# A two-layer encoder trunk on one core: recurrence levels in 32-column blocks, and weight splits in another order

## The reference

```python
def hgrn2(h, w_in, lb, o_norm_g, w_out):
    q, f, i, g = jnp.split(h @ w_in, 4, axis=-1)
    forget = lb + (1.0 - lb) * jax.nn.sigmoid(f)
    k, q = 1.0 - forget, jax.nn.silu(q)
    # S_t = diag(f_t) S_{t-1} + k_t i_t^T,  o_t = S_t^T q_t, with 8 heads of 128
    ...
    return (rms_norm(o) * jax.nn.silu(g)) @ w_out

def moe_swiglu(h, w_router, b_router, w_gu, w_down):
    # the two best of 8 experts for each token
    for e in range(N_EXPERTS):
        out = out + gates[..., e:e + 1] * swiglu(h, w_gu[e], w_down[e])   # E_FF = 3584
```

## Time and profile before

| | us |
|---|---|
| median of 3 runs | 1499.53 (1497.72 to 1499.70) |
| the profiled execution | 1497.92 |
| its span | 1496.2 |
| PE busy | 1465.4 |
| DVE busy | 1237.6 |
| ACT busy | 1004.9 |

### The profile page before, as it was taken

One profiled execution on the slowest core, in us unless ns is written; L12 is line 12 of the kernel. 1 busy time (PEld: TensorE's weight loads), 2 busy tenths in 40 slices (PEclk: granted clock), 3 DMA queues, 4 the chain that ended last, 5 costly groups with the idle time before them and its releaser, 6 DMA issues.

```text
span 1496.2 us, 23664 instructions
## 1 busy us (share of the span) xinstructions
PE 1465.4 (98%) x6903; PEld 1215.8 (81%) x6903; DVE 1237.6 (83%) x1556; ACT 1004.9 (67%) x1248; POOL 45.9 (3%) x43
## 2 busy tenths in 40 slices
PE   8999999999999999999999999999999999999998
PEld 6877888788887778888888888888888888888876
DVE  7996545674778899899989989889989889899985
ACT  6555434366236677787877877777787778778762
POOL 1000000000000120000000000000000000000000
PEclk9999999999999999999999999999999999999999
DMA  7666555456233899999999999999989999999960
GB/s 284 210 219 224 188 199 174 168 167 213 74 128 122 299 410 409 346 367 409 347 374 410 356 364 410 387 327 411 403 319 408 409 341 381 409 348 399 410 245 29
DMA packets 124631, 452.57 MB, mean 302 GB/s; under 512 B 13984, under 2 KB 13984, under 8 KB 124592
## 3 DMA queue, kind: packets, MB, share of 16 engines
q1 hardware_dynamic: 119952, 435.25, 77.4%
q0 software_dynamic: 4640, 16.82, 3.1%
HBM read 443.62 MB, written 8.39 MB: 302 GB/s over the span
## 4 chain that ended last, share of the span: by engine, by line
PE 89%; DVE 7%; issue 1%; ACT 1%; DMA 1%; SPq 0%; ACTq 0%; DVEq 0%
PE PS L460 28%; PE PS L462 28%; PE PS L461 28%; DVE w_lo L1362 3%; PE PS L880 2%; DMA raw<-in_w_in_ab 1%; PE PS L511 0%; PE PS L726 0%; DVE SC L1666 0%; PE PS L847 0%; ACT w_hi L984 0%; DVE SC L1685 0%; DVE SC L1686 0%; PE PS L597 0%; PE PS L834 0%
## 5 line engine op out<-in xcount | busy, mean ns | idle before, releaser
L1362 DVE TENSOR_TENSOR w_lo<-raw,w_hi 128x1024 fp32r<-128x1024 f32 x486 | 568.6, 1221 | 31.4 <-ACT w_hi L984 28.4
L460 PE MATMUL PS<-w_hi,xT_hi 128*128 128x512 f32 x1424 | 567.5, 399 | 6.1 <-DVE w_lo L1362 3.4
L462 PE MATMUL PS<-w_lo,xT_hi 128*128 128x512 f32 x1424 | 557.5, 392 | 0.0
L461 PE MATMUL PS<-w_hi,xT_lo 128*128 128x512 f32 x1424 | 556.4, 391 | 0.0
L984 ACT ACTIVATE w_hi<-raw 128x1024 fp32r<-128x1024 f32 x486 | 489.6, 1060 | 73.0 <-PE PS L462 41.8
L1362 DVE TENSOR_TENSOR w_lo<-SC,w_hi 128x1024 fp32r<-128x1024 f32 x340 | 392.0, 1220 | 8.4 <-ACT w_hi L984 6.8
L984 ACT ACTIVATE w_hi<-SC 128x1024 fp32r<-128x1024 f32 x340 | 335.7, 1061 | 12.3 <-PE PS L462 10.3
L460 PEld LDWEIGHTS PS<-w_hi,xT_hi 128*128 128x128 f32 x1424 | 269.5, 189 | 60.7 <-issue 6.3
L462 PEld LDWEIGHTS PS<-w_lo,xT_hi 128*128 128x128 f32 x1424 | 268.6, 189 | 57.8
L461 PEld LDWEIGHTS PS<-w_hi,xT_lo 128*128 128x128 f32 x1424 | 269.2, 189 | 52.9
L460 PE MATMUL PS<-w_hi,hT_hi 128*128 128x512 f32 x536 | 209.1, 390 | 3.2 <-DVE hT_lo L1580 3.2
(11 more groups left out here) (270 smaller groups left out, 625.8 us busy)
## 6 DMA issues: line engine op xcount, KB each, us to landing
raw<-in_e_w_gu SPq DMA_DIRECT2D x226, 512.0 KB, 8.5
SC<-in_e_w_gu SPq DMA_DIRECT2D x222, 512.0 KB, 8.3
SC<-in_e_w_down SPq DMA_DIRECT2D x114, 512.0 KB, 7.5
raw<-in_e_w_down SPq DMA_DIRECT2D x110, 512.0 KB, 7.8
raw<-in_ffn_w_gu SPq DMA_DIRECT2D x44, 512.0 KB, 4.8
raw<-in_w_in_c SPq DMA_DIRECT2D x32, 512.0 KB, 6.0
raw<-in_ffn_w_down SPq DMA_DIRECT2D x22, 512.0 KB, 5.1
raw<-in_w_in_ab SPq DMA_DIRECT2D x20, 512.0 KB, 8.5
```

Of the source, the lines that this page charges most:

```text
L460: pe.matmul(out, a_hi, b_hi, start=start, stop=False, skip_group_check=True)
L461: pe.matmul(out, a_lo, b_hi, start=False, stop=False, skip_group_check=True)
L462: return pe.matmul(out, a_hi, b_lo, start=False, stop=stop, skip_group_check=True)
L1362: dve.tensor_tensor(w_lo[:, g % RING, part], raw_part(g, s), w_hi[:, g % RING, part].bitcast(F32), ALU.subtract).then_inc(lo_done, 1)
```

## The change

The levels 0 to 5 are cut into four blocks of 32 stationary columns (in the order 0, 64, 32, 96), each with 32 moving columns in level 0 and 16 in levels 1 to 5. The splits of 64 and 65 stand before level 0's merge, 66 behind level 6's update, 67 and 68 behind level 7's, 69 to 72 each where 70 to 73 stood, 73 where 74 stood, and 74 ahead of the first expert's `xg`. In the experts' unit, h is made behind the first of three splits.

```diff
             def level(n):
                 pe.wait_ge(qk_ready, n + 1)
                 for hd in range(HEADS):
                     for t in range(T):
-                        tok = slice(t * P, (t + 1) * P)
-                        if n == 0:
-                            c = (hd % 2) * SEQ + t * P
-                            m = pe.matmul(PS[:, 4 + hd // 2, c:c + P], kT[:, hd, tok], qT[:, hd, tok],
-                                          start=True, stop=True, skip_group_check=True)
+                        if n < 6:
+                            for a in (0, 2 * B, B, 3 * B):
+                                rows, tok = slice(a, a + B), slice(t * P + a, t * P + a + B)
+                                if n == 0:
+                                    c = (hd % 2) * SEQ + t * P + a
+                                    m = pe.matmul(PS[rows, 4 + hd // 2, c:c + B], kT[:, hd, tok], qT[:, hd, tok],
+                                                  start=True, stop=True, skip_group_check=True)
+                                else:
+                                    w = 2 ** (n - 1)
+                                    c = (hd % 4 * T + t) * (P // 2) + a // 2
+                                    m = pe.matmul(
+                                        PS[rows, level_bank(n) + hd // 4, c:c + B // 2].rearrange("p (m w) -> p m w", w=w),
+                                        kT[:, hd, tok], qT[:, hd, tok].rearrange("p (m e w) -> p m e w", e=2, w=w)[:, :, 1, :],
+                                        start=True, stop=True, skip_group_check=True)
...
-            los(62, 64)
+            los(62, 65)
             dve.wait_ge(qT_act, 4)
             dve.sem_inc(qk_ready, 1)
+            lo(65)
...
             meet(0)
             step(dve.tensor_tensor(qT, qT, fT, ALU.mult))
             dve.sem_inc(qk_ready, 1)
-            lo(64)
...
-                if 1 < lv < 7:
-                    lo(63 + lv)
+                if lv == 6:
+                    lo(66)
+            los(67, 69)
...
             norm_o(0)
+            lo(69)
+            gate_o(0)
             lo(70)
-            gate_o(0)
-            lo(71)
...
             gate_o(1)
+            lo(71)
+            xT(1, 4, V_ON)
             lo(72)
-            xT(1, 4, V_ON)
-            lo(73)
...
-            lo(74)
+            lo(73)
...
             select(1)
+            lo(74)
             xg(1)
...
                 def unit(u, end):
-                    for q in (10, 11, 12):
-                        lo(G_MOE + q, i * EU + u)
+                    lo(G_MOE + 10, i * EU + u)
                     unit_hidden(i * EU + u + (FB + 2))
+                    lo(G_MOE + 11, i * EU + u)
+                    lo(G_MOE + 12, i * EU + u)
```

More of the change, by code:

```diff
@@ L697, in turn_heads @@
                         m.then_inc(signal, 1)
+            B = 32
             def level(n):
@@ L722, in level @@
                                               skip_group_check=True)
[L723 to L729, removed]
                 m.then_inc(at_done, 1)
```

## The result

The changed kernel took 1501.32 us in the median against 1498.98 for the kernel before, timed on the same chip: ratio 1.0015, 95% interval 1.0009 to 1.0022, +2.3 us. The interval leaves out 1, so this is a small loss, of 1.3 to 3.3 us; 1501.4 had been forecast. The two profiled executions took 1497.92 before and 1502.34 after (spans 1496.2 and 1500.6, 4.4 apart), so the single profiles differ by 2 us more than the medians do; 0.5 of it is there before the first level already.

A forecast was written before the change was run, and what follows sets the result against it. PE, busy 98% of the span, was taken to bound the kernel. Terms -5.8 (recurrence), -4.3 (first item), +9.1 (item ends) and +2.9 (last unit) sum to +1.9 us: 1501.4 from a median of 1499.53, range 1495.0 to 1507.0.

The forecast's parts named there:

- three signs by which I wanted to be wrong: No wait at the boundaries; PE standing in the levels longer than 1.0 us; PE's granted clock falling inside the levels.
- rival A: Recurrence levels: narrow passes and waits lower PE's clock, +2 to +4 us, hence 1503.5 to 1505.5; chance 0.20.
- Levels: Levels 0 to 5: 2.2 us each instead of 3.49, bounds 1.2 and 3.49; level 7 at 414.0 instead of 424.72.
- rival D: Levels 0 to 5: four column groups side by side, 1.2 us a level, level 7 2.6 earlier, 1498.8; chance 0.10.
- The stall in front of the weighting: Before the weighting of values: PE stands 5.4 us for split 66, load 69, ACT's cast and copies; start 424.3, not 431.13.
- The clock: Behind the stall before the weighting: PE's clock low again, 1.0 us charged, as 12 matmuls lost after the old stall.
- Cost zero: Later splits, 74 ahead of expert 0's xT: covered by 2.25 us of DVE idling; 2.3 were that cover absent.
- First item: Expert stage, first item: h made when split 82 ends, 522.5, ahead of PE's want at 525.1; gain 4.3 us.
- Item ends: Seven expert boundaries: two splits stand between h and the next xT, PE waits 1.3 us each; loss 9.1.
- Last unit: Last expert unit: pT's low part and hT come two splits later, hT ends at 1454.9; loss 2.9 us (2 to 4).
- Rival C: Expert boundaries: no wait for xT, so the 9.1 us loss goes away, 1492.3; chance 0.12.
- Rival B: Levels 0 to 5: nothing saved, 3.49 us each, PE bounds again, level 7 at about 420, 1507.4; chance 0.08.

The follow-up runs named there:

- same_group: Changed kernel with h behind three splits, and in levels 0 to 5 the 16 products of one column block one behind the other: 1502.55 us, ratio 1.0032.
- cast69_later: Changed kernel with ACT's cast of granule 69 behind its copies of levels 6 and 7, not ahead of them: 1495.35 us, ratio 0.9983.
- levels_and_product: Kernel before with the 32-column blocks in levels 0 to 5 and the h placement of three_at_end, splits staying in the levels: 1485.45 us, ratio 0.9911.
- three_cast: three_at_end and cast69_later together: 1482.92 us, ratio 0.9903 against the kernel before.
- split74_behind: three_cast with split 74 behind the tokens of expert 0 on DVE: 1486.39 us, ratio 0.9927 against the kernel before.
- xg_first: Changed kernel with the next expert's xT (in the last unit pT) directly behind h, ahead of two splits: 1499.98 us, ratio 1.0016.
- three_at_end: Changed kernel with h behind one split only in looped units of items before the last, behind three elsewhere: 1485.98 us, ratio 0.9920.
- levels_only: Kernel before with only the 32-column blocks of levels 0 to 5: 1490.64 us, ratio 0.9956.
- splits_only: Kernel before with only the splits moved, levels at 128 columns and h behind three splits: 1500.58 us, ratio 1.0019.

## Why the prediction was right

The time came out within 0.1 us and the difference of the medians as +2.3 for +1.9, and the terms of -5.8, -4.3, +9.1 and +2.9 were measured as -5.2, -4.5, +9.8 and +4.8. Each of the four has the sign and the mechanism that were forecast. The near hit of the sum owes much to luck. The four terms add up to +4.9 and not +1.9, and a cost that I had put at nothing is +1.9 more; two places where the clock happened to do better than before (-1.4 and -1.6) take 3.0 off, one of them tied to that cost. Between the profiles the difference is still +4.4, 2.1 more than between the medians. The base moved too, from 1499.53 (3 runs) to 1498.98 (19).

Two of the three signs by which I wanted to be wrong did show: PE stood in the levels longer than 1.0 (1.69 in front of level 3), and its clock fell inside them (0.74). Neither had the effect that I had tied to it, as the paragraphs on the levels and on rival A show.

**Levels: too long by a factor of 1.8, and little of it reached the total.** I took 2.2 a level from level 6. It was 1.20, my lower bound, the size of rival D: four column groups run side by side (*same_group*). (My 16 ns a pass for level 6 rests on 1.04 us, which the earlier trace rows do not show; their 1.14 makes it 18.) The Trainium skill's sentence on starts no closer than about 25 ns (TensorE: Matmul & The Clock Gate, "Wait — 56ns, not 53.3ns?") does not hold for products in different groups, at 9.4 ns a pass, and stands close to what was measured within one group, 30 ns. Part 3 of the same page, Packing small matmuls, was the section that bore on this case. As far as level 7 rival D was the right one. DVE set the pace around level 3, where PE stood 1.69 and not 1.0, but level 7 came at 412.00 for my 414.0, or 2.5 earlier counted from level 0, where D had 2.6. D's time, 1498.8, did not come because only 1.2 of this reached the weighting, and the clock there cost 1.8 more than I charged (both below).

**The stall in front of the weighting: right mechanism, 6.60 for 5.4.** Split 66 ended at 414.9, 1.5 earlier than forecast, but the second half of load 69 was taken by the cast at 420.31, only 0.6 earlier, since w_out_c now took 5.4 in the median of eight and not the 4.3 of the earlier trace rows. So of D's 2.6 only 0.7 arrived, 1.2 counted from level 0: the weighting began at 423.62 for my 424.3. Why the load was slower was not tried; in the other profiles its median is 4.0 to 5.9. That ACT's cast is the link was shown by *cast69_later*.

**The clock: 1.0 charged, 2.8 measured.** From the weighting's start to the next projection matmul it was 6.26 (423.62 to 429.88), before 3.49 (431.13 to 434.62). I had priced the low clock by the projection's matmuls behind the old stall. Now it fell on the weighting's products, whose first 16 passes show 3.75 and not 1.95. Counted from level 0, the weighting began 1.2 earlier than forecast, which makes up for most of it: -5.2 for -5.8.

**"Cost zero" for split 74: wrong in this profile, +1.9 from gather to first h.** PE waits 1.63 for the tokens, and the clock over the next 9 us is 0.81. The step that failed is the cover. I let the split fill the 2.25 that DVE idled ahead of the tokens, but these belong to a profile whose gather ran at a low clock and took 4.18. Where the gather takes 3.73, as after, only 0.57 are left with the old order (*levels_and_product*), and a split of 2.36 makes the tokens some 1.7 late, an estimate from these rows. Nine profiles have split 74 ahead of the tokens: the two with a gather of 3.73 (after and *three_cast*) show the wait, 1.63 and 1.62, and the seven with one of 3.89 to 5.23 show none. So the +1.9 and most of the -1.4 ahead of the gather belong together: the clock that saved the one laid the split bare. *split74_behind* keeps the split between the gather and the first h and only moves it behind the tokens, where it makes that h late.

**First item: 4.5 for 4.3.** The second turn comes 17.43 after the first and the third 16.84 after that, against 20.23 and 18.53.

**Item ends: 1.40 each for 1.3, 9.8 for 9.1.** The wait for xT is where I put it, 120.65 us apart (the profile's 1.15 counts from the end of the transposes before it). DVE's timeline after, of one item's end:

```profile
601.20 0.69 DVE L1875 TENSOR_TENSOR junk<-junk,PS 128x512 f32<-128x512 f32 x1 [2.78 <-ACT junk L1258]
...
606.34 2.16 DVE L1828 SCALAR_TENSOR_TENSOR xT_lo<-PS,vcol,xT_hi 128x128 fp32r<-128x128 f32 x8
...
622.69 0.69 DVE L1875 TENSOR_TENSOR junk<-junk,PS 128x512 f32<-128x512 f32 x1
```

h starts at 601.20, two splits follow, and the first four of xT end 6.2 later, for the 6.28 of the prediction. What I had not seen is that this is one of two waits with one cause. I worked out that the next h would be ready 22.2 after this h starts and wanted at 22.7; measured 22.2 (622.69 and 0.69, less 601.20) and 22.9 (624.07). That margin existed only because the wait for xT had moved PE back. With xT made first, PE wants h at 21.6 and the loss is 1.2 all the same (*xg_first*). Rival C is refuted for the change, and *three_at_end* shows what it takes to be rid of the loss: the wait for silu must be filled with splits.

**Last unit: 4.8 for 2.9.** hT was made when forecast: its instruction on DVE ends 0.2 before PE takes it at 1456.43, at 1456.2, which less the 1.1 that all stands later there is 1455.1 for my 1454.9. The size failed at the clock: behind the second of two waits, 1.37 and 2.23, the next eight matmuls start 0.43 apart and not 0.23, some 1.6 us. The window after shows the clock (seventh number):

```profile
1456.00:1464.00 8.00, 7.51 (x25) 5.76 (x26) 3.15 (x4) 0.81 (x2) 0.00 (x0) 0.79 0.00 0
```

**Rival A came true in part and cost nothing.** In the profile after the clock over 393 to 399.5 is 0.74. Yet level 4 starts 5.74 behind level 3 (393.67 to 399.41), and in *three_at_end*, whose clock was 1.00 there, 5.75 (394.75 to 400.50) with a wait of 1.50. The slow matmuls filled a wait for DVE. The clock fell there in one of eight profiles with a wait of 1.6 to 1.7 in front of level 3; behind the 3.80 of *levels_only* it fell too (0.57 over 401 to 405). **Rival B** is excluded by the 1.20. *splits_only* has B's recurrence without the new place of h: level 7 comes 44.96 behind level 0, B's "about 420", and the kernel took 1500.6, to which the product's 10.6 would be added.

## What to carry to other kernels

Ask of work that is moved off an engine's path which idle time it filled where it stood: the splits ahead of h filled the wait for silu, and putting h first left DVE idle for 2.8 us at each item's end (1.0 before) and PE for 1.4, seven times; in the recurrence the moved splits only carried the stall from DVE's updates to a load. An operation that waits for a transfer should not stand in an in-order queue ahead of one that others wait for: two casts, moved a few places down, won 8.7 us together. Narrow products should go round the column groups in turn, and each long PE wait should be charged with the clock behind it at the price of the very instructions that run there.

## What the runs showed of the hardware that was not expected

- 128-row float32 products of 32 stationary columns cost 30, 18 and 9.4 ns a pass with one, two and four column groups in turn. The order of one loop was worth 2.65 us a level; blocks of 32 columns in the wrong order (3.85) are slower than 128 columns at once (3.49).
- With four times as many matmuls PE stood once with nothing to wait for that the profile shows ("issue"), for 0.18 to 0.85 us in level 1 or 2, as below from the profile after. Seven of the ten profiles whose blocks go round the column groups have such a gap, at a place that differs. What makes it was not tried.

```profile
384.54 0.32 PE L716 MATMUL PS<-SC 128*32 128x16 f32 x15 [0.73 <-issue]
```

- Between the last two turns of the program the same work takes 8.2 us in some kernels' profiles and 9.5 to 9.9 in others'. In the kernel before, with 9.8, the clock between them was 0.83 (0.71 over 1465 to 1470), and after, with 8.2, it was 1.00. No part of the change touches this place, so 1.6 us of a difference between two single profiles can be this alone. Why it falls in one and not the other stays open.
